# Experts' up weights in 2-MB loads of paired rows, and another order of work in the conditioning phase of a decoder layer

## The reference

```
mod = silu(c) @ ada_w + ada_b                       # 6 x 1024: shift1, scale1, gate1, shift2, scale2, gate2
h   = rms_norm(x, norm_mix_w) * (1 + scale1) + shift1
x   = x + gate1 * hybrid_mixer(h)                   # h @ w_in, then latent attention and RWKV-7, merged, @ w_out
h   = rms_norm(x, norm_ffn_w) * (1 + scale2) + shift2
# top 4 of 32 experts for each token; each expert with its tokens:
gu  = xb @ w_gate_up[e] + b_gate_up[e]              # 1024 -> 2048
gate, up = min(gu[:, 0::2], 7), clip(gu[:, 1::2], -7, 7)
y   = ((up + 1) * gate * sigmoid(1.702 * gate)) @ w_down[e] + b_down[e]
x   = x + gate2 * sum over a token's experts of weight * y
```

## Time and profile before

| what | us |
|---|---|
| median of three runs (1694.9 to 1696.96) | 1696.89 |
| the profiled execution | 1690.92 |
| its span in the profile | 1689.1 |
| second phase's first matmul | 56.26 |
| first turn's transposes in the experts' loop | 612.42 |
| last turn's transposes | 1653.22 |
| PE busy | 1624.8 (96%) |
| one load of 1 MB of `w_gate_up`, mean from issue to landing | 20.7 |

### The profile page before, as it was taken

The page is one execution under the profiler, slowest core; times in us unless marked ns, Lnnn a source line. Parts: engine busy times, 40 slices in busy tenths (PEclk is TensorE's granted clock), DMA queues, the critical chain, the costliest instruction groups (busy, mean ns, idle before and its releaser), DMA issues.

```text
span 1689.1 us, 44996 instructions
## 1 busy us (share of the span) xinstructions
PE 1624.8 (96%) x19080; PEld 900.9 (53%) x19080; DVE 573.7 (34%) x1333; ACT 423.7 (25%) x869; POOL 282.8 (17%) x355
## 2 busy tenths in 40 slices
PE   7999897999999989999999999999999999999996
PEld 5658797677888843334434433443443344334333
DVE  0539374655334544113212211321222132122212
ACT  3343433575223402111112111111211111111111
POOL 4000530101000020221211122112212212121211
PEclk9999999999999979999999999999999999999998
DMA  9860000222222399999999999999999999999983
GB/s 367 321 245 1 2 5 5 102 79 100 102 98 100 133 359 380 410 396 403 400 393 398 401 397 394 400 395 387 406 394 393 390 402 398 388 396 390 399 340 128
DMA packets 87472, 489.68 MB, mean 290 GB/s; under 512 B 15093, under 2 KB 17202, under 8 KB 34504
## 3 DMA queue, kind: packets, MB, share of 16 engines
q1 hardware_dynamic: 77260, 470.76, 69.9%
q0 software_dynamic: 7504, 16.80, 4.2%
q10 hardware_dynamic: 2636, 1.08, 0.3%
HBM read 478.61 MB, written 19.55 MB: 295 GB/s over the span
## 4 chain that ended last, share of the span: by engine, by line
PE 54%; DMA 7%; SPq 1%; DVE 0%; issue 0%; POOLq 0%; DVEq 0%
PE bank L2266 33%; PE bank L2277 17%; DMA sb_w_raw<-in_w_gate_up_dram 7%; SPq L1840 1%; PE bank L2257 1%; PE bank L2290 1%; PE bank L2278 1%; PE bank L2267 1%; DVE sb_y L2493 0%; PE bank L2305 0%; PE bank L2300 0%; DVE sb_biased L2474 0%; POOLq L2157 0%; PE bank L2310 0%; DVE sb_aT L2470 0%
## 5 line engine op out<-in xcount | busy, mean ns | idle before, releaser
L2266 PE MATMUL bank<-sb_w_raw,sb_xT 128*32 128x512 f32 x4608 | 673.5, 593 | 4.1 <-DMA sb_w_raw<-in_w_gate_up_dram 3.5
L2267 PE MATMUL bank<-sb_w_raw,sb_xT 128*32 128x512 f32 x1536 | 672.5, 593 | 0.0
L2266 PEld LDWEIGHTS bank<-sb_w_raw,sb_xT 128*32 128x32 f32 x4608 | 185.2, 110 | 440.9 <-issue 417.4
L2277 PE MATMUL bank<-sb_w_raw,sb_aT 128*32 128x256 f32 x4608 | 337.9, 379 | 2.0 <-DVE sb_aT L2471 2.0
L2278 PE MATMUL bank<-sb_w_raw,sb_aT 128*32 128x256 f32 x1536 | 337.5, 380 | 0.0
L2277 PEld LDWEIGHTS bank<-sb_w_raw,sb_aT 128*32 128x32 f32 x4608 | 187.7, 110 | 130.9 <-DVE sb_y L2493 2.3
L2474 DVE TENSOR_TENSOR sb_biased<-bank,sb_bias 128x512 f32<-128x512 f32 x96 | 60.4, 685 | 482.4 <-PE bank L2267 369.8
L2278 PEld LDWEIGHTS bank<-sb_w_raw,sb_aT 128*32 128x32 f32 x1536 | 166.3, 110 | 0.0
L2267 PEld LDWEIGHTS bank<-sb_w_raw,sb_xT 128*32 128x32 f32 x1536 | 165.3, 110 | 0.0
L2372 ACT COPY sb_bias<-sb_last_quarter 32x1536 f32<-32x1536 f32 x32 | 47.0, 1469 | 402.5 <-POOL sb_last_quarter L2429 402.5
L2424 POOL TENSOR_TENSOR sb_tick<-sb_ones 128x1 f32<-128x1 f32 x93 | 34.0, 366 | 559.3 <-issue 410.7
(11 more groups left out here) (491 smaller groups left out, 2227.9 us busy)
## 6 DMA issues: line engine op xcount, KB each, us to landing
sb_w_raw<-in_w_gate_up_dram SPq DMA_DIRECT2D x256, 1024.0 KB, 20.7
sb_w_raw<-in_w_down_dram SPq DMA_DIRECT2D x128, 1024.0 KB, 21.9
sb_ring<-in_w_in_dram SPq DMA_DIRECT2D x7, 2048.0 KB, 13.6
sb_x<-in_ada_w_dram SPq DMA_DIRECT2D x8, 1024.0 KB, 9.5
sb_mod<-in_ada_w_dram SPq DMA_DIRECT2D x8, 1024.0 KB, 8.2
sb_ring<-in_ada_w_dram SPq DMA_DIRECT2D x6, 1024.0 KB, 15.2
sb_x<-in_x_dram SPq DMA_DIRECT2D x2, 2048.0 KB, 10.4
sb_ring<-in_w_out_dram SPq DMA_DIRECT2D x2, 2048.0 KB, 8.0
```

The source lines that it names most:

```text
L2266: te.matmul(up_bank[r][at, :], g.xT[:, k, at], g.w_raw[:, s, 512 * r:512 * r + 512], start=first, stop=last)
L2267: mm = te.matmul(up_bank[r][CAP:P, :], g.xT[:, k, STRIP * r:STRIP * r + STRIP], g.w_raw[:, s, 512 * G:2048], start=first, stop=last)
L2277: te.matmul(down_bank[j][at, 0:256], g.aT[:, k, at], g.w_raw[:, s, 1024 * r + 256 * j:1024 * r + 256 * j + 256], start=first, stop=last)
```

## The change

*Experts.* `load_up` moves two blocks at once: rows 128k to 128k + 255 of `w_gate_up`, 2 MB, into two neighbouring slots, and partition p gets rows 2p and 2p + 1 of them, 16 KB in one run. SP waits until both slots have been used, PE waits once for each pair. The features of a pair of blocks are therefore interleaved, so `features` reads `x_slot` with a step of two elements, and the scale and shift columns come in the same order from a new tile `mod_pairs`, loaded by two small DMAs in the output phase.

*Conditioning.* The nine small loads go from ACT's stream to the end of SP's in this phase; the wait for them moves from DVE's end of the phase to PE in the projection. The cast `first_hi` moves ahead of the copy of the columns. ACT writes the rounded features `hT` from the bank at once, DVE writes the exact ones `h32` from the same bank, and the low half of the first weights in four pieces; PE takes these low products within the loop over k. There are more fillers: 3 ahead of the columns, 9 behind them, 4 before the last low products. The eight subtractions that give `h_lo` move to the beginning of the projection on DVE; PE begins that phase with 4 fillers and the eight hi x hi products of r0, then takes each `h_lo` block as it comes, then the rest of r0. SP stores `h_lo` when the last of them is there.

```diff
 def load_up(g, sp, s, e, k):
-    src = g.a["w_gate_up"][0][e, P * k:P * k + P, :]
-    sp.dma_start(g.w_raw[:, s, :], src.rearrange("a p n -> p (a n)")).then_inc(g.raw_in[s], 16)
+    src = g.a["w_gate_up"][0][e, P * k:P * k + 2 * P, :]
+    sp.dma_start(g.w_raw[:, s:s + 2, :].rearrange("p a n -> p (a n)"), src.rearrange("a (p r) n -> p (a r n)", r=2)).then_inc(g.raw_in[s], 16)
...
             def rest_of_turn(turn, e, after):
-                for k in range(SPARE, UP):
+                for k in range(SPARE, UP, 2):
                     sp.wait_ge(*was_used(up_slot(k), turn))
+                    sp.wait_ge(*was_used(up_slot(k + 1), turn))
                     load_up(g, sp, up_slot(k), bass.ds(after, 1), k)
...
-                    mm = te.transpose(turn_bank[i][:, CAP * j:CAP * j + CAP], g.x_slot[0:CAP, P * k:P * k + P], g.ident[0:CAP, 0:CAP])
+                    pair = g.x_slot[0:CAP, P * (k - k % 2):P * (k - k % 2) + 2 * P].rearrange("p (n r) -> p r n", r=2)
+                    mm = te.transpose(turn_bank[i][:, CAP * j:CAP * j + CAP], pair[:, k % 2, :], g.ident[0:CAP, 0:CAP])
...
-                    te.wait_ge(*loaded(up_slot(k), turn))
+                    if k % 2 == 0:
+                        te.wait_ge(*up_loaded(up_slot(k), turn))
...
+            for i in range(2):
+                pairs = g.mod_rows[0, 1 + i, :].rearrange("(k p r) -> p k r", p=P, r=2)
+                sp.dma_start(g.mod_pairs[:, i, :].rearrange("p (k r) -> p k r", r=2), pairs, allow_slow_non_contiguous=True).then_inc(g.pairs_in, 16)
...
-                sc.activation(g.h32[:, k, :], turned(k), ACT.Identity, bias=g.mod1_cols[:, k:k + 1], scale=g.gain[:, k:k + 1]).then_inc(*act(f"h{k}"))
+                sc.activation(g.hT[:, k, :], turned(k), ACT.Identity, bias=g.mod1_cols[:, k:k + 1], scale=g.gain[:, k:k + 1]).then_inc(*act(f"h{k}"))
...
+            keep_busy(3)
             te.wait_ge(*vec.at("mod"))
             for i in range(4):
                 mm = te.matmul(ps[COLS][:, i:2 * KD:4], g.mod1[:, P * i:P * i + P], g.ident[:, 0:P:STRIP], start=True, stop=True)
             mm.then_inc(*pe("mcol"))
+            keep_busy(9)
             te.wait_ge(*vec.at("w_hi"))
             for k in ks:
-                te.wait_ge(*vec.at(f"hh{k}"))
+                te.wait_ge(*act.at(f"h{k}"))
                 for i in range(2):
                     te.matmul(ps[i][:, :], g.first_hi[:, i, k, :], g.hT[:, k, :], start=(k == 0), stop=False)
                 if k < HALF_K:
                     features(k + HALF_K)
-            te.wait_ge(*vec.at("w_lo"))
-            for i in range(2):
-                for k in ks:
-                    te.matmul(ps[i][:, :], low_slot(g, LO)[:, k, P * i:P * i + P], g.hT[:, k, :], start=False, stop=False)
+                if k % 2:
+                    if k == KD - 1:
+                        for _ in range(4):
+                            te.matmul(ps[SUMS][:, 0:P], g.ones[:, :], g.ones[:, :], start=True, stop=True)
+                    te.wait_ge(*vec.at(f"w_lo{k // 2}"))
+                    for j in (k - 1, k):
+                        for i in range(2):
+                            te.matmul(ps[i][:, :], low_slot(g, LO)[:, j, P * i:P * i + P], g.hT[:, j, :], start=False, stop=False)
```

More of the change, by code:

```diff
@@ L203, in phase_adaln @@
         HALF_K = KD // 2
-        vec = g.steps(ctx, "a_vec", ["rows", "zero", "cols", "cond", "rstd", "mod", "mcol", "gain", "w_hi"] + names("hh{}", KD) + ["w_lo"] + names("hl{}", KD))
+        vec = g.steps(ctx, "a_vec", ["rows", "zero", "cols", "cond", "rstd", "mod", "w_hi", "mcol", "gain"]
+                      + [x for k in ks for x in [f"hx{k}"] + ([f"w_lo{k // 2}"] if k % 2 else [])])
         act = g.steps(ctx, "a_act", ["sig", "sq0", "sq1", "sq2", "sq3", "std"] + names("xn{}", NT) + names("h{}", KD))
@@ L298, in _ @@
             ve.tensor_tensor(g.mod1[:, :], ps[SUMS][:, :], g.ada_b[:, :], ALU.add).then_inc(*vec("mod"))
+            ve.wait_ge(*chunk_loaded(g, LO))
+            raw = slot(g, LO).rearrange("p k (i n) -> p i k n", i=2)
+            ve.tensor_copy(g.first_hi[:, :, :, :], raw).then_inc(*vec("w_hi"))
             ve.wait_ge(*pe.at("mcol"))
@@ L535, in late @@
                 conditioned(te, g, g.ps[SUMS], h % KD, late_place(g, h % 4)).then_inc(*pe(f"late{h}"))
-            for i in range(2):
-                for k in range(KD):
-                    mm = te.matmul(bank[f"l{i}"][:, :], g.first_hi[:, i, k, :], g.h_lo[k], start=False, stop=(k == KD - 1))
-                mm.then_inc(*pe(f"l{i}"))
+            for _ in range(4):
+                te.matmul(g.ps[SUMS][:, 0:P], g.ones[:, :], g.ones[:, :], start=True, stop=True)
+            te.wait_ge(*act.at("w0"))
+            for k in range(KD):
+                te.matmul(bank["r0"][:, :], g.w_hi[:, 0, k, :], g.hT[:, k, :], start=(k == 0), stop=False)
+            for k in range(KD):
+                te.wait_ge(*vec.at(f"hl{k}"))
+                for i in range(2):
+                    mm = te.matmul(bank[f"l{i}"][:, :], g.first_hi[:, i, k, :], g.h_lo[k], start=False, stop=(k == KD - 1))
+                    if k == KD - 1:
+                        mm.then_inc(*pe(f"l{i}"))
+            for k in range(KD):
+                te.matmul(bank["r0"][:, :], g.w_hi[:, 0, k, :], g.h_lo[k], start=False, stop=False)
+            te.wait_ge(*vec.at("w0"))
+            for k in range(KD):
+                mm = te.matmul(bank["r0"][:, :], low_slot(g, RKV)[:, k, 0:P], g.hT[:, k, :], start=False, stop=(k == KD - 1))
+            mm.then_inc(*pe("r0"))
             for i in f4:
-                feature(f"r{i}", RKV, i)
+                if i:
+                    feature(f"r{i}", RKV, i)
                 late(2 * i)
@@ L2202, in down_slot, with up_loaded, down_loaded @@
             return SPARE + q
-        def loaded(s, turn):
+        def up_loaded(s, turn):
             return raw_in[s], 16 * turn + (16 if s >= UP else 32)
+        def down_loaded(s, turn):
+            return raw_in[s], 16 * turn + (16 if s % 2 else 32)
         def was_used(s, turn):
@@ L2238, in _ @@
                 e, after = expert(sp, turn), expert(sp, turn + 1)
-                for k in range(SPARE):
+                for k in range(0, SPARE, 2):
                     sp.wait_ge(*was_used(up_slot(k), turn))
+                    sp.wait_ge(*was_used(up_slot(k + 1), turn))
                     load_up(g, sp, up_slot(k), bass.ds(after, 1), k)
@@ L2344, in _ @@
                 for q in range(DOWN):
-                    te.wait_ge(*loaded(down_slot(q), turn))
+                    te.wait_ge(*down_loaded(down_slot(q), turn))
                     down(down_slot(q), q).then_inc(used[down_slot(q)], 1)
@@ L2360, in features_copy @@
                 for k in range(4):
-                    mm = sc.activation(g.xT[:, k, :], turn_bank[0][:, CAP * k:CAP * k + CAP], ACT.Identity, scale=g.mod_cols[:, 1, k:k + 1], bias=g.mod_cols[:, 0, k:k + 1])
+                    mm = sc.activation(g.xT[:, k, :], turn_bank[0][:, CAP * k:CAP * k + CAP], ACT.Identity, scale=g.mod_pairs[:, 1, k:k + 1], bias=g.mod_pairs[:, 0, k:k + 1])
                 return mm
```

65 lines of the change are left out of this document (35 added, 30 removed).

## The result

The changed kernel takes 1698.95 us (median of 20 runs, 1694.86 to 1704.06), the kernel before in the same rounds 1694.32 (1689.14 to 1698.78). The ratio is 1.0032, 95% interval 1.0022 to 1.0042: it is slower by about 5 us. The forecast of 1688 lies 6 us under the kernel before in these rounds, and its sum promised 9 us. The runs of either kernel spread over 9 us, and the trace of before that the prediction read (1690.92) lies at the fast end of them.

A forecast was written before the change was run, and what follows sets the result against it. The prediction took the experts' loop to be bound by PE and loads nearly meeting (32.85 and 33.62 us a turn), plus waits at the start. 1690.92 - 4.3 (start) - 4.7 (loop) = 1681.9, plus 5.97 gives 1688; range 1683 to 1696.

The forecast's parts named there:

- The term of the 2-MB loads: Experts' loop: paired loads with 16-KB packets shrink the 5.4 us lost to loads; -4.7 us.
- the price of a pair: Experts' loads: one 16-KB packet at 0.614 us replaces two 8-KB ones at 0.310 each, saving 0.006 to 0.008 us.
- R4: Experts' loads: DMA engines cut 16-KB runs in two, packet count stays, time as R1's; chance 0.12 together with R1.
- R1: Experts' loads: packets pay nothing, only later refill remains, up to 2.7 us; 1692.6 to 1695.3; chance 0.12 with R4.
- The stride: Experts' transposes: reading x_slot at every second element costs nothing, covered by other work; upper end +13 us.
- R3: Experts' transposes: strided loads stand open on PE, making it slower, +13 to +48 us (1701 to 1736); chance 0.09.
- The start: Conditioning up to phase two: five steps together gain -4.3 us, between -2.3 and -5.8.
- (a): Start: nine small loads moved to SP's end let squares begin when x lands; -3.5 us, bounds -2.46 to -4.5.
- (b): Start: w_hi's cast moves ahead of the columns' copy, nine more fillers follow the columns; +0.37 us.
- (c): Start, first to last product: features written at once, low half in quarters, DVE's work covered by PE; -1.42 us.
- (d): Start, barrier before phase two: PE is last instead of DVE's subtraction; -0.83 us.
- (e): Start of phase two: eight subtractions move there on DVE, covered by PE's products after four fillers; +1.07 us.

The follow-up runs named there:

- e3: The whole change, but tokens' rows stored once in paired order so the loop's transposes read without a stride, against the kernel before: ratio 1.0038.
- e4: The whole change, but 2-MB loads in 8-KB packets (rows p and p + 128) and transposes without a stride, against the kernel before: ratio 1.0046.
- e1: The conditioning part of the change alone, experts' loop as before, against the kernel before: ratio 0.9974.
- e5: e1, but SP waits for two neighbouring up slots, then issues two 1-MB loads; against the kernel before: ratio 0.9989.
- e11: e8 with strided transposes and 1-MB loads that take every second row of 256; against the kernel before: ratio 1.0003.
- e7: The kernel before with only the nine small loads moved to SP's end and their wait to the projection: ratio 0.9972 to the kernel before.
- e6: The kernel before, unchanged, traced a second time: its loop takes 1042.2 us from first to last transposes.
- e2: The experts' part of the change alone, start as before, against the kernel before: ratio 1.0035.
- e8: e1 without the twenty fillers that the change adds, against the kernel before: ratio 0.9959.
- e9: e8 with each 1-MB up block loaded by two DMAs of 64 partitions, 8-KB packets: 2578 us.
- e10: e8 with 16-KB packets, a pair of slots filled by two 1-MB DMAs of 64 partitions, no stride in the transposes: six runs, 2540 to 2642 us.

## Why the prediction was wrong

**What bounds the kernel** was read rightly: two limits that nearly meet, PE's 32.85 us a turn and the loads' 33.62, with a reserve that is used up after some 22 turns. What wasn't drawn from it is how steep that makes the loop. With the reserve used up before the end, whatever makes a turn's loads longer is paid in each of some 30 turns: 0.3 us a turn is 9 us.

**The term of the 2-MB loads** was -4.7 and is +9 to +14 in the loop by e3 and e4, 11 to 12 us by their ratios against e1 (nothing by e5 for the refill alone). The step that failed is the price of a pair: it was to save some 0.007 us, and 32 of them with the semaphore writes 0.27 us a turn, so that the loads would need 32.85 + 0.53 = 33.38 us. They need 33.92. The price came from the earlier trace rows, a stretch of 10 us and a broadcast outside the loop. By the packets' own times in the traces, from 700 to 1100 us, an 8-KB packet takes 0.323 us in the kernel before, a 16-KB packet 0.656 in the changed one, not 0.614: a pair costs 0.010 us more. In e3 it takes 0.646, neither more nor less than two of 8 KB, and the loads need 33.9 us all the same, so the mean time of a packet doesn't tell all of it. SP's queue in the DMA views of that stretch, before, then the changed kernel:

```profile
q1 hardware_dynamic: 21041, 153.22, 94.6%
```

```profile
q1 hardware_dynamic: 13849, 151.14, 93.9%
```

That is 39.5 us of engine time for 1 MB before (94.6% of 16 x 400 us for 153.22 MB) and 39.8 now. The packets are fewer, so nothing cuts a run of 16 KB in two, and R4 falls. R1 stood near the outcome, with the right sign and the wrong mechanism and size: its price was the refill's 2.7.

**The stride** was taken at nothing, with 51 ns as the upper end and 34 ns as the point from which it decides. It is 40 ns a transpose (1.13 - 0.81 over 8) and comes fully into the turn, 33.17 against 32.85. R3's mechanism was real, near its lower price. But its decision point was worked out as if costs on PE went straight to the end, and in the change it adds nothing to the loads' loss (e3 against the changed kernel). In e11 it comes with 7 us, of which 2 to 3 are its own by the estimate there. The Trainium skill's note on cachelines (SBUF — State Buffer, section "Door 1"), by which a stride of two fp32 costs nothing, is contradicted by the trace for a PE weight load: 216 ns against 141.

**The start** was -4.3 and is -9.2 at the second phase's first matmul (47.05 against 56.26), -8.1 at the projection's last late conditioning product (111.87 against 119.93). The forecast was too small in three of its five steps. (a) The columns' matmuls come 6.0 us earlier (33.28 against 39.27), not 3.5; e7, with this one edit, has them at 33.37. The wait of 2.46 went, and with it the low clock that followed it: PE was idle until 31.28 us, and 32 to 39 us ran at 0.77 of the clock before, the same work now at 1.00.

```profile
32.00:39.00 7.00, 6.38 (x40) 3.92 (x39) 0.48 (x1) 0.00 (x0) 0.00 (x0) 0.77 1.09 369
```

```profile
26.00:33.00 7.00, 7.00 (x61) 5.04 (x59) 0.47 (x1) 0.00 (x0) 0.79 (x4) 1.00 1.04 373
```

(The first row is of before, the second of the changed kernel; the seventh number, behind the five busy times, is the clock.) (b) -0.2 for +0.37; (c) 10.28 us from 36.20 to 46.48, so -2.5 for -1.42; (d) 0.57 in place of 1.16, -0.6 for -0.83; (e) +1.1 for +1.07, with no wait shown for the subtractions. So (a) and (c) were too small, (b) had the wrong sign, (d) and (e) were about right.

**What the start is worth at the end** is the step that was missing. The sum was carried to the end as if the 550 us in between kept all of it. e1 keeps 4.4 us of its 8. Most of the loss lies in the recurrence's chunks, code that no edit touches. From their first matmul to the first behind them it takes 107.8, 109.6 and 111.0 us with the old start (before, e6, e2; 109.5 in the mean), 110.1 in e7, and 110.4 to 113.8 with the new start in seven traces (112.4 in the mean). In this stretch PE has waits that nothing in the program explains. Before, then e6, then the changed kernel, one wait each:

```profile
282.19 0.27 PE L966 MATMUL bank<-sb_ring 64*64 64x64 f32 x2 [1.26 <-issue]
```

```profile
283.40 0.27 PE L966 MATMUL bank<-sb_ring 64*64 64x64 f32 x2 [1.81 <-issue]
```

```profile
270.46 0.27 PE L971 MATMUL bank<-sb_ring,sb_x 64*64 64x64 f32 x1 [1.91 <-issue]
```

No engine and no data ends these waits, and in the DMA view of the stretch (before, 264 to 286 us) nothing moves but instruction loads, six in 22 us:

```profile
DMA packets 6, 0.10 MB, mean 4 GB/s; under 512 B 0, under 2 KB 0, under 8 KB 0
...
q8 instruction: 6, 0.10, 1.8%
```

Each of the six is 16 KB in one packet of about 1 us. The first five end at 267.01, 270.69, 274.06, 277.52 and 280.87 us, and PE is idle from 267.02, 270.51, 274.24, 277.59 and 280.93 us on. I read that as PE waiting for its own code; the trace doesn't name the engine that the code is for. The same instruction waits 1.26 us in one trace of before and 1.81 in the other. In five of the seven traces with the new start, and in e7, a stretch of 3.4 or 6.8 us at half the clock falls into the chunks as well (e1 and e8 at 190 us), in the three with the old start none does. So some 3 of the start's 8 us went into a stretch that varies from run to run, and which the first trace of before had at its shortest. Whether the new start makes it longer or the three traces of the old one were lucky isn't settled.

**The form of the sum.** -4.3 - 4.7 became, at the loop's first transposes, about -4 (609.4 in the mean of five traces with the new start and its fillers, 613.7 in three with the old), then +10 in the loop, and +5.4 was measured. The forecast's base was 2.6 us too high as well: 1696.89 by three runs, 1694.32 in the rounds of the comparison.

**What stays open:** why the loads of e3, e4 and the changed kernel are slower than two of 1 MB that are issued back to back into the same slots. That they are, e4 against e5 shows. That it is the size of the DMA isn't shown: the loads of e11 are of 1 MB, but each reaches over the same 2 MB of rows, and they need 33.9 us a turn too. The trace adds one thing. A load's semaphore is raised sixteen times, and in the kernel before, from 680 to 1100 us, the ninth of them comes about 11 us after the issue all along, while the last gets later by 0.65 us a turn (up weights); in e4 the ninth, too, gets later, by 0.33, and the last by 1.02. So a part of each load falls behind and the rest keeps up, which a mean busy share of 1.00 doesn't show. e9 and e10, made to go on from there, met another limit.

## What to carry to other kernels

Where a loop's compute and its loads take nearly the same time and a reserve covers the difference, price a change to the loads as its effect on one turn's loads times the number of turns, and take that effect from a run of that very form of DMA, not from single packets elsewhere. A cost that is hidden under another one's waits shows only when each is tried without the other: here the pair loads cost about 10 us with the stride and without it, and the stride's 0.32 us a turn counts only where loads don't set the end. The edit that paid was the smallest: taking nine small DMA issues out of the engine that the first chain waits for. With the rest of the new start, without its fillers and with the old loop (e8), the kernel is 0.41% faster than before and 0.7% faster than the change; from e7, with that one edit, it can't be told.

## What the runs showed of the hardware

- In a queue that is never empty, the landing of DMAs of 2 MB to 128 partitions gets later by 1.1 us in a turn of 12 MB (e3, e4), that of pairs of 1 MB by 0.8 (e5, e1). The loop takes 1051 to 1056 us against 1041 to 1043. DMAs of 1 MB that take every second row of 2 MB are slow as well (e11).
- A packet of 16 KB takes 0.646 us (e3) to 0.656 us (the changed kernel) in the loop, one of 8 KB 0.323 us in that of the kernel before: the longer run saves nothing.
- With the up weights loaded by DMAs to 64 of the 128 partitions, the engines move little over half: 233 GB/s with packets of 8 KB (e9) and 224 with 16 KB (e10), against 397.
- A PE weight load whose source has a step of two fp32 takes 216 ns in place of 141, and the pitch of a row of transposes goes from 0.10 to 0.14 us.
- Where PE runs small products of 64 x 64, it is idle for 1.2 to 1.9 us behind each of the loads of code (16 KB), and the wait differs from run to run with the same code (1.26 and 1.81 us at one instruction).
